# Two windowed and dense attentions: the products with the values of unit n-2 moved in front of the turning of unit n-1

## The reference, cut to what matters

```python
def dense_attention(q, k, v):
    scale = q.shape[-1] ** -0.5
    s = jnp.einsum('bqhd,bkhd->bhqk', q, k).astype(jnp.float32) * scale
    p = jax.nn.softmax(s, -1).astype(v.dtype)
    return jnp.einsum('bhqk,bkhd->bqhd', p, v)
```

```python
        s_loc = jnp.einsum('bchd,bicjhd->bhcij', q_row, k_win).astype(jnp.float32) * scale + bias.astype(jnp.float32)
        s_ctx = jnp.einsum('bchd,bnhd->bhcn', q_row, k_ctx).astype(jnp.float32) * scale
...
        p = jax.nn.softmax(s, -1).astype(v.dtype)
        o = jnp.einsum('bhcij,bicjhd->bchd', p[..., :n_loc].reshape(B, H, GRID_W, kh, kw), v_win)
        return o + jnp.einsum('bhcn,bnhd->bchd', p[..., n_loc:], v_ctx)
```

## Time and profile before

| | |
|---|---|
| Time, median of 3 runs (lowest to highest) | 3968.15 us (3963.56 to 3971.21) |
| The profiled execution: its time, its span | 3967.02 us, 3965.3 us |
| Busy: PE, DVE, ACT | 3403.0 us (86%), 1159.6 us (29%), 677.9 us (17%) |
| Latent attention: S of the first and of the last unit | 1585.3 us, 1733.4 us |
| Neighbourhood attention: S of the first and of the last unit | 3252.6 us, 3327.6 us |

### The profile page before, as it was taken

One profiled execution on the slowest core, in us unless ns is written; L12 is line 12 of the kernel. 1 busy time (PEld: TensorE's weight loads), 2 busy tenths in 40 slices (PEclk: granted clock), 3 DMA queues, 4 the chain that ended last, 5 costly groups with the idle time before them and its releaser, 6 DMA issues. The chain is left out here.

```text
span 3965.3 us, 50846 instructions
## 1 busy us (share of the span) xinstructions
PE 3403.0 (86%) x21532; PEld 1980.0 (50%) x21532; DVE 1159.6 (29%) x2238; ACT 677.9 (17%) x1295; POOL 334.3 (8%) x463
## 2 busy tenths in 40 slices
PE   6999998999969899896799996997777899587776
PEld 3767476565524555676333332556666446322222
DVE  2214222323322176654100000345454235300000
ACT  1105012102110134421100001213130022100000
POOL 0000000000000000000111111134633000000000
PEclk9999999999989999997899998997776999699999
DMA  3210222433471200104899997301002110599999
GB/s 120 80 65 3 100 81 87 159 126 117 160 246 48 89 7 0 33 12 160 302 394 395 395 397 270 117 27 23 18 12 86 69 52 21 214 389 400 403 403 355
DMA packets 276742, 637.93 MB, mean 161 GB/s; under 512 B 65300, under 2 KB 128100, under 8 KB 269222
## 3 DMA queue, kind: packets, MB, share of 16 engines
q1 hardware_dynamic: 266470, 611.61, 41.6%
q0 software_dynamic: 10048, 23.07, 2.5%
HBM read 593.59 MB, written 41.05 MB: 160 GB/s over the span
## 5 line engine op out<-in xcount | busy, mean ns | idle before, releaser
L391 PE MATMUL bank<-weights_l,hT_l 128*128 128x256 f32 (+3 forms) x1552 | 477.5, 475 | 11.5 <-ACT values_l L321 4.4
L391 PEld LDWEIGHTS bank<-weights_l,hT_l 128*128 128x128 f32 (+1 forms) x1552 | 334.6, 221 | 152.2 <-issue 76.9
L1881 PE MATMUL bank<-expert_weights_l,expert_tokensT_l 128*32 128x512 f32 x3072 | 339.5, 598 | 10.8 <-DMA expert_weights_l<-in_moe_w 9.2
L2087 PE MATMUL bank<-expert_weights_l,expert_tokensT_l 128*64 128x512 f32 x1024 | 242.8, 622 | 80.7 <-DMA expert_weights_l<-in_moe_w 79.6
L386 PE MATMUL bank<-hT_l,weights_l 128*128 128x512 f32 (+1 forms) x832 | 288.6, 510 | 0.8 <-DVE padded_l L2932 0.8
L386 PEld LDWEIGHTS bank<-hT_l,weights_l 128*128 128x128 f32 x832 | 161.8, 195 | 125.8 <-issue 114.9
L1881 PEld LDWEIGHTS bank<-expert_weights_l,expert_tokensT_l 128*32 128x32 f32 x3072 | 106.6, 111 | 229.0 <-issue 228.0
L1755 POOL DMA_INDIRECT expert_rows_l<-normed_rows,row_numbers_l x16 | 15.4, 961 | 2312.5 <-DMA row_numbers_l<-selected_rows 2308.2
L1312 PE MATMUL bank<-hT_l,gate_weights_r 128*128 128x512 f32 x384 | 198.6, 645 | 5.2 <-ACT gate_rows_r L1319 4.7
L2087 PEld LDWEIGHTS bank<-expert_weights_l,expert_tokensT_l 128*64 128x64 f32 x1024 | 80.3, 142 | 232.6 <-issue 179.4
L1916 PE MATMUL bank<-expert_weights_l,rows 128*32 128x512 f32 x1536 | 167.9, 592 | 0.9 <-ACT rows L1956 0.9
(11 more groups left out here) (530 smaller groups left out, 4624.6 us busy)
## 6 DMA issues: line engine op xcount, KB each, us to landing
expert_weights_l<-in_moe_w SPq DMA_DIRECT2D x192, 2048.0 KB, 25.1
ada_weights_r<-in_ada_w SPq DMA_DIRECT2D x48, 1024.0 KB, 5.0
weights_l<-in_w_in SPq DMA_DIRECT2D x9, 2048.0 KB, 7.9
weights_l<-in_w_in SPq DMA_DIRECT2D x15, 1024.0 KB, 5.2
gate_weights_r<-in_w_in SPq DMA_DIRECT2D x24, 512.0 KB, 5.6
weights_l<-in_od_w_in SPq DMA_DIRECT2D x7, 1024.0 KB, 5.8
gate<-gate_rows_r SPq DMA_DIRECT2D x24, 256.0 KB, 5.6
weights_l<-in_ev_w_in SPq DMA_DIRECT2D x3, 2048.0 KB, 8.5
```

The lines of the kernel that those rows point to most:

```text
L391: ins = pe.matmul(bank[r:r + x.shape[1], :n], x, w_sb[:, k, :n], start=k == 0, stop=k == kt - 1)
L1881: return pe.matmul(bank[q * STRIP:(q + 1) * STRIP, :], xs[:, k, e, g * STRIP:(g + 1) * STRIP], w[:, j, h * HALF:(h + 1) * HALF], start=k = ...
L2087: ins = pe.matmul(bank[h * S:h * S + S, :], rows(k), ring[r][:, k % DEEP, h * HALF:(h + 1) * HALF], start=k == 0, stop=k == KT - 1)
```

## The change

In each round of the loop two calls change places with two others; no instruction and no wait is added or removed.

```diff
@@ -2507,12 +2507,12 @@
             scores_pe(n)
             max_dve(n)
             exp_act(n)
+        if n >= 2:
+            values_pe(n - 2)
+            out_dve(n - 2)
         if 1 <= n <= N:
             turn_pe(n - 1)
             turned(n - 1)
-        if n >= 2:
-            values_pe(n - 2)
-            out_dve(n - 2)
         if between:
             between(n)
```

## The result

| | before | changed |
|---|---|---|
| Time, median (lowest to highest, runs) | 3969.68 us (3963.56 to 3975.81, 6) | 3993.85 us (3986.80 to 3999.17, 6) |
| Span of the profiled execution | 3965.3 us | 3992.6 us |
| Busy: PE, DVE, ACT | 3403.0, 1159.6, 677.9 us | 3409.5, 1162.6, 679.4 us |

The changed kernel is slower by 0.62% (ratio 1.0062, 95% interval 1.0050 to 1.0074), 24 us. The forecast was 3985 with a range of 3970 to 3995. The engines run the same instructions.

The account below looks back on a forecast made before the run. The prediction took the latent loop as close to bound by PE, with short waits to win. Latent +7.7 and neighbourhood +10 gave +17.7 us on 3967.0, so 3984.7, forecast as 3985; the 8-in-10 range was 3970 to 3995.

Parts of the forecast that it names:

- The exchange of waits: Behind S(n), PE meets V(n-2) waiting for copies instead of T(n-1) waiting for exponentials; T itself no longer waits.
- the signs named: V waits 20 us or more in the latent attention, some 12 in the neighbourhood; engine work unchanged, clock at 1.00.
- Latent, a regular head: Each regular latent head 0.91 to 1.18 us longer, from V's waits in the rounds of tiles 4, 1 and 5.
- The loop: Whole latent loop +7.7 us: six regular heads 6.3, the first two heads 0.4, the end 1.
- a wait of tile 5: Latent head, round of tile 5: V of tile 3 newly waits 0.36 to 0.45 us for its DVE copy.
- the first two heads: Latent start: the other branch's stages on DVE and ACT set the pace; nothing to 2.4 us, say 0.4.
- Neighbourhood: Whole neighbourhood loop 8.8 to 11.5 us longer, say 10, from V's waits for copies and its end.
- The window: Neighbourhood: the next head's window, behind copy and division, starts 0.2 to 0.3 us later, delaying V of tile 3 equally.
- the step on the clock: Both loops: new waits of about 1.2 us at most in one round cost only themselves, without a clock loss.
- The third rival: One wait in each of 16 heads halves the clock for some 3 us of work: 48 us more, 4033; 5 in 100.
- fill the wait: Rival: V(n-2) is ready when PE comes, T's waits vanish: 13 us gained in the latent attention, 3954; 6 in 100.
- No change: Rival: waits only change their name; two ACT steps per latent head remain, 5 us: 3968 to 3974; 14 in 100.

Follow-up runs that it names:

- exponentials behind the copy: Changed kernel, but on ACT the exponentials of unit n come after the copy of unit n-1; 3976.34 us, ratio 1.0022 to the kernel before.
- V of n-3: Against the changed kernel, products and division one round later (unit n-3), still in front of T of n-1; 3951.02 us, ratio 0.9959 to the kernel before.
- old order at the end: Changed kernel with T in front of V again in the last three rounds of each loop; 3982.85 us, ratio 1.0034 to the kernel before.
- latent only: Kernel before with the new order in the latent attention alone; 3980.68 us, ratio 1.0034.
- V of n-3 behind T: Kernel before with its order kept (T, then V), but products of unit n-3 instead of n-2; 3965.10 us, ratio 0.9995.
- neighbourhood only: Kernel before with the new order in the neighbourhood attention alone; 3978.32 us, ratio 1.0031.

## Why the prediction was right, and what it missed

*The exchange of waits* was right. V stands where T stood, and waits for a copy that ACT takes up behind the exponentials. That this queue decides in the latent heads is shown by the run with the exponentials behind the copy, and that the nearness of T and V decides by the run with V of n-3. Of the signs named, V's waits of 20 us or more in the latent attention came (22.1); the 12 us of the neighbourhood attention did not (5.6 and 0.9 in the view, which misses the shorter ones).

*Latent, a regular head*: forecast +0.91 to +1.18 us, measured 18.10 - 17.04 = +1.06 (17.04 is 1679.20 - 1662.16: in the trace before, S of tile 4 of the next head starts at 1679.20). The single waits fit: in the round of tile 4 V comes 4.63 - 4.33 = 0.30 us later than T did (0.28 to 0.37), from the end of the ACT copy to V it is 0.14 us (taken as 0.06 to 0.15), from T to V in the round of tile 5 1.50 us (1.51 to 1.60). *The loop*: forecast +7.7, measured +9.0. From the first matmul of S to the last it grew from 148.3 to 154.9 us, 6.6; the rest, 2.4, lies behind it, up to the last V (3.2 us before, 5.6 after), where I had put 1 and a wait of tile 5. The end of the loop was sized too small, and so were the first two heads: 46.4 us before and 47.3 after, +0.9 where I had put 0.4.

*Neighbourhood*: forecast +10, measured +8.6 and +8.8. A head grew by 1.00 us; the terms gave 1.06 to 1.34. The window was late by 0.88 - 0.67 = 0.2 us, the lower end of what I had taken. The waits of V for tiles 2, 0 and 1 came out at 0.25, 0.20 and 0.19 us, where I had 0.30 to 0.39, 0.25 to 0.34 and 0.18 to 0.27: from T to its copy it is 0.71 us (3287.85 to 3288.56), and I had taken 0.79.

*Sum of the loops*: forecast +17.7, measured +17.6 and +17.8. That it is so close is luck in part: the latent loop came out 1.3 us over its term, the other 1.2 to 1.4 under.

*What failed* is the step on the clock: "By these rows the new waits, 0.86 + 0.36, about 1.2 us, at most in one round, cost only themselves." In the regular heads that holds: the granted clock is 1.00 from 1640 to 1720 us with waits of 1.27 us in every head. At the drained ends it does not: there several waits follow one another with little work between, the clock falls to half, and the ways behind the loops take 2.3 and 2.7 to 4.0 us more. These 5.0 to 6.3 us, which the sum had at nothing, are most of the 9 us by which the time came out over the forecast; another 1.5 is the kernel before, whose median was 3969.68 us in these runs and 3968.15 in the earlier ones, and the rest cannot be told from chance. That the measured time still lies in the range, near its upper end, is owed to the width of other terms; no term was for the clock at the ends. The third rival had the clock fall in every head, for 48 us; it happened at two places, the ends, for 5.0 us together in the first traces and 6.3 in the second. (In the second latent head, too, the granted clock was 0.79 from 1612 to 1620 us in the changed kernel, behind a wait of V of 1.67 us, and 1.00 before; what that cost is within the 0.9 us of the first two heads.)

The Trainium skill ("TensorE: Matmul & The Clock Gate", section "A second HAM failure mode: psum-queue depth-cycling") says that short idle gaps between groups of matmuls can make the clock fall and rise again. In the regular heads no row here shows that. At the two ends of the loops the rows above show one fall and one return, after waits of 0.60 to 0.94 us.

*The other rivals.* V did not fill the wait in a regular latent head, as the ACT copies ended after the exponentials. "No change" failed on the waits of tile 5 and of the neighbourhood attention, which arose, though a little shorter than forecast.

## What to carry to other kernels

Before work is moved forward to fill a wait, look whether its own inputs are ready at that moment: the row to read is the end of the instruction that makes them, and its place in the queue of its engine, not the end of the one that is waited for now. In a loop that is pipelined over several engines, an exchange in the order and a greater distance between producer and consumer belong together; here each alone gave nothing or a loss in the time of the kernel, both together a gain of 0.4%. The drained end of such a loop deserves its own look, since waits there may cost the clock of what follows.

## What the runs showed of the hardware that was not expected

- Behind both loops of the changed kernel the granted clock was 0.62 and 0.52 over 8 us, so that part of them ran at the half level, though the waits of V in the last rounds were short: 0.60 to 0.73 us in the latent attention, 0.67 to 0.94 us in the other. The waits of a regular latent head, 0.62, 0.25 and 1.27 us within 18 us, left it at 1.00. What the engine did before it fell: in the latent attention three V in a row had waited (they start at 1739.28, 1742.50 and 1744.98 us) and the last one was waiting; in the other attention there were waits of 0.90 and 0.94 us, 2.5 us apart. The 8 us at these ends had 5.76 and 6.08 us of PE work. With the old order at the end the latent loop still had two waits, of 0.62 and 0.64 us, 3.3 us apart, and the clock stayed at 1.00.
- The step from a wide S to what follows takes 1.29 us when V follows (S at 1659.04, V at 1660.33 in the changed kernel) and 1.34 when T does. The forecast had bounded such steps at 0.05 us either way and taken them as nothing; the difference is at that bound.
- In the first 8 us of the neighbourhood loop the granted clock was 1.00 in six traces (the two kernels twice each, latent only, V of n-3 behind T) and 0.77 to 0.79 in the five others, though the kernel with the old order at the end has the same order there as the changed one, and PE is busy as long (5.76 and 5.78 us of the 8). Where the clock fell for such a stage, the first head took some 1.5 us more (neighbourhood only, 10.85 against 9.36). What decides whether it falls there is not shown.
